# A two-part transformer kernel on one core: gate and modulation work split and counted through, and stages that begin with the high part of h

## The reference

```python
for i in range(DEPTH):                      # first stack, 2 layers
    a = rms_norm(h, attn_norm[i])
    proj = a @ w_in[i]                      # split: attention, state space and gated linear mixers
    h = h + mix @ w_out[i]
    f = rms_norm(h, ffn_norm[i])
    h = h + (silu(f @ w_ffn_gate[i]) * (f @ w_ffn_up[i])) @ w_ffn_down[i]
    h = h + sigmoid(h @ ple_w_gate[i]) * (p[i] @ ple_w_proj[i])
c_act = silu(c)
for i in range(DEPTH_2):                    # second stack, 4 layers
    mod = c_act @ ada_w[i] + ada_b[i]       # 1024 x 6144, a matrix-vector product
    sh1, sc1, g1, sh2, sc2, g2 = split(mod, 6)
    h = rms_norm(x, norm_gain[i, 0]) * (1.0 + sc1) + sh1
    x = x + g1 * attention_i(h)             # stick-breaking, block, sliding window, stick-breaking
    h = rms_norm(x, norm_gain[i, 1]) * (1.0 + sc2) + sh2
    x = x + g2 * swiglu(h, ffn_w_gate[i], ffn_w_up[i], ffn_w_down[i])
```

## Time and profile before

| | |
|---|---|
| runs | 2368.3, 2370.2, 2378.3 us; median 2370.16 us |
| the profiled execution | 2372.31 us, of which the span from first to last instruction is 2370.5 us |
| mean granted clock of TensorE | 0.971 of 2.4 GHz |
| TensorE busy | 2210.4 us (93%), 17460 matmul records |
| DVE, ACT busy | 1573.5 us (66%), 1072.2 us (45%) |
| moved from memory | 433.82 MB, 183 GB/s over the span |

### The profile page before, as it was taken

One profiled execution on the slowest core, in us unless ns is written; L12 is line 12 of the kernel. 1 busy time (PEld: TensorE's weight loads), 2 busy tenths in 40 slices (PEclk: granted clock), 3 DMA queues, 4 the chain that ended last, 5 costly groups with the idle time before them and its releaser, 6 DMA issues.

```text
span 2370.5 us, 44905 instructions
## 1 busy us (share of the span) xinstructions
PE 2210.4 (93%) x17460; PEld 2080.8 (88%) x17460; DVE 1573.5 (66%) x2623; ACT 1072.2 (45%) x1728; POOL 0.2 (0%) x4
## 2 busy tenths in 40 slices
PE   5889999898999999999899999899988999998998
PEld 4778899877888999799899888799877999897998
DVE  4676678726766888366788766778777555676554
ACT  3545444324454443255444445544455444555443
POOL 0000000000000000000000000000000000000000
PEclk7999999999999999899999999999999999999999
DMA  4465399834552998454599753599842565542764
GB/s 119 110 161 159 112 301 292 270 111 122 156 152 88 304 303 281 123 160 132 160 296 305 242 147 113 169 297 301 262 116 90 160 186 168 143 142 76 206 188 142
DMA packets 549150, 436.34 MB, mean 184 GB/s; under 512 B 27664, under 2 KB 475192, under 8 KB 548920
## 3 DMA queue, kind: packets, MB, share of 16 engines
q1 hardware_dynamic: 545680, 431.22, 59.8%
q10 hardware_dynamic: 3368, 3.71, 0.5%
HBM read 433.82 MB, written 1.05 MB: 183 GB/s over the span
## 4 chain that ended last, share of the span: by engine, by line
PE 80%; DVE 9%; ACT 4%; DMA 2%; DVEq 2%; issue 1%; ACTq 1%; SPq 0%
PE bank L633 14%; PE bank L635 13%; PE bank L634 13%; PE acc L633 7%; PE acc L635 6%; PE acc L634 6%; PE bank L1225 3%; PE bank L756 3%; PE bank L1133 2%; PE bank L816 2%; PE bank L643 1%; ACT w_hi L1258 1%; DVE head_work L1666 1%; DVE w_lo L1691 1%; PE bank L826 1%
## 5 line engine op out<-in xcount | busy, mean ns | idle before, releaser
L633 PE MATMUL bank<-h_hi,w_hi 128*128 128x256 f32 x3024 | 862.3, 285 | 26.8 <-DVE w_lo L1685 9.9
L634 PE MATMUL bank<-h_lo,w_hi 128*128 128x256 f32 x3024 | 843.8, 279 | 0.0
L635 PE MATMUL bank<-h_hi,w_lo 128*128 128x256 f32 x3024 | 843.7, 279 | 0.0
L1258 ACT ACTIVATE w_hi<-wslot 128x1024 fp32r<-128x1024 f32 x574 | 594.0, 1055 | 508.4 <-PE acc L635 265.9
L1691 DVE TENSOR_TENSOR w_lo<-wslot,w_hi 128x1024 fp32r<-128x1024 f32 x396 | 475.1, 1221 | 224.5 <-ACT w_hi L1258 223.9
L633 PEld LDWEIGHTS bank<-h_hi,w_hi 128*128 128x128 f32 x3024 | 569.8, 188 | 54.5 <-DVE w_lo L1685 15.9
L634 PEld LDWEIGHTS bank<-h_lo,w_hi 128*128 128x128 f32 x3024 | 573.7, 190 | 2.3 <-issue 1.7
L635 PEld LDWEIGHTS bank<-h_hi,w_lo 128*128 128x128 f32 x3024 | 570.9, 189 | 0.0
L633 PE MATMUL acc<-mid_hi,w_hi 128*128 128x256 f32 x1120 | 316.9, 283 | 4.3 <-DVE mid_lo L2032 3.3
L635 PE MATMUL acc<-mid_hi,w_lo 128*128 128x256 f32 x1120 | 312.3, 279 | 0.0
L634 PE MATMUL acc<-mid_lo,w_hi 128*128 128x256 f32 x1120 | 312.3, 279 | 0.0
(11 more groups left out here) (274 smaller groups left out, 2629.0 us busy)
## 6 DMA issues: line engine op xcount, KB each, us to landing
wslot<-in_ada_w_dram SPq DMA_DIRECT2D x192, 512.0 KB, 5.9
wslot<-in_ffn_w_gate_dram SPq DMA_DIRECT2D x88, 512.0 KB, 4.8
wslot<-in_ffn_w_up_dram SPq DMA_DIRECT2D x88, 512.0 KB, 5.4
wslot<-in_ffn_w_down_dram SPq DMA_DIRECT2D x88, 512.0 KB, 3.7
wslot<-in_w_in_dram SPq DMA_DIRECT2D x72, 512.0 KB, 5.0
wslot<-in_sb_w_in_dram SPq DMA_DIRECT2D x48, 512.0 KB, 4.6
wslot<-in_w_ffn_gate_dram SPq DMA_DIRECT2D x44, 512.0 KB, 4.8
wslot<-in_w_ffn_up_dram SPq DMA_DIRECT2D x44, 512.0 KB, 5.5
```

The lines of the kernel that those rows point to most:

```text
L633: pe.matmul(dst, w_hi[:, w, cols], hi, start=start, stop=False, skip_group_check=True)
L634: pe.matmul(dst, w_hi[:, w, cols], lo, start=False, stop=False, skip_group_check=True)
L635: return pe.matmul(dst, w_lo[:, w, cols], hi, start=False, stop=stop, skip_group_check=True)
L1258: return act.activation(dst, src, ACT.Copy)
```

## The change

- Modulation blocks are numbered through over all four layers, 48 in all. Each `ffn` does 11 (`ADA_STEPS`) until they are used up: 11, 11, 11, 11, 4 and 0. The phases `ada_units` and `ada_end` are gone; a phase `modulation` after each `ffn`'s add stores the last block and makes `mod_gain`.
- The gate products are split like the others. The eight gate units come in slots 0, 1, 8 and 9, the projection weights as two whole units in slots 2 and 3. The first two gate units and both projection units are loaded ahead of the last gate and up unit of `ffn`, p is turned inside `ffn` too, and the first two gate units are split at its end. In the gate stage TensorE does all projections first, into the four banks, then the gate tiles into `acc`; the first two tiles go along together as quarters of h are split. Each tile is added to `xT` as it is ready.
- At the start of every attention and every `ffn` the first tiles go along together, tile of h by tile of h, and for each the products with the high part come first, on `h_high`, and those with the low part after, on `h_parts`.

```diff
+PLE_SLOTS = (0, 1, 8, 9, 0, 1, 8, 9)
+PLE_PARTS = (0, 1, 3, 4, 2, 0, 1, 3)
+def ada_blocks(ada):
+    return max(0, min(ADA_STEPS, DEPTH_2 * ADA_BLOCKS - ADA_STEPS * ada))
...
+            def first_tiles(g, tiles):
+                for k in range(KT):
+                    pe.wait_ge(sem["h_high"], g("h_high") - KT + k + 1)
+                    for dst, part, first in tiles:
+                        pe.matmul(dst, w_hi[:, part, k_cols(k)], h_hi[:, k, :], start=(first and k == 0), stop=False, skip_group_check=True)
+                        pe.matmul(dst, w_lo[:, part, k_cols(k)], h_hi[:, k, :], start=False, stop=False, skip_group_check=True)
+                    pe.wait_ge(sem["h_parts"], g("h_parts") - KT + k + 1)
+                    for n, (dst, part, _) in enumerate(tiles):
+                        mm = pe.matmul(dst, w_hi[:, part, k_cols(k)], h_lo[:, k, :], start=False, stop=(k == KT - 1), skip_group_check=True)
...
-                project(0, 0)
-                project(0, 1)
+                first_query(g)
...
-                elif kind == "ada_end":
-                    ada_sum(ph["start"], ADA_BLOCKS - 1)
...
-                        for k in range(KT):
-                            mm = pe.matmul(B(2 * b, 0, 256), wk(s, k), xT[:, k, :], start=(k == 0),
-                                           stop=(k == KT - 1))
+                    for m in range(KT):
+                        if m == KT - 2:
+                            pe.wait_ge(sem["ada_stored"], g("ada_stored"))
+                        for n in range(2):
+                            mm = pe.matmul(B(m // 2, 256 * (m % 2), 256 * (m % 2) + 256), wk(SLOT_PROJ + n, m),
+                                           qk[:, 256 * n:256 * n + 256], start=(n == 0), stop=(n == 1))
...
+                        mm = three(acc[:, 2 * (m % 4) + m // 4, :], PLE_PARTS[m], k_cols(k), h_hi[:, k, :], h_lo[:, k, :],
+                                   k == 0, k == KT - 1)
...
+                    for k in range(KT):
+                        if k % 2 == 0:
+                            pe.wait_ge(sem["h_parts"], g("h_parts") + k + 2)
+                        gate(0, k)
+                        gate(1, k)
...
-                    with dve.Fori(0, KT // 2) as i:
+                    for m in range(KT):
+                        gated = silu_g[:, m % 2, :]
+                        dve.wait_ge(sem["ple_s"], g("ple_s") + m + 1)
+                        dve.tensor_tensor(gated, gated, B(m // 2, 256 * (m % 2), 256 * (m % 2) + 256), ALU.mult)
+                        dve.drain()
+                        last = dve.tensor_tensor(xT[:, m, :], xT[:, m, :], gated, ALU.add)
```

More of the change, by code:

```diff
@@ L137, in mix_prior, with runs @@
     return max([v for v in range(u) if mix_part(v) == mix_part(u)], default=None)
+def runs(kinds, lo):
+    ends = [i for i in range(lo + 1, len(kinds)) if kinds[i] != kinds[i - 1]]
+    return list(zip([lo] + ends, ends + [len(kinds)]))
 def grouping(att, n):
@@ L2226, in _, with step @@
                     ada = ph["ada"]
-                    def step(f, b, i, more=True, waits=True, first=False):
+                    def step(f, b, i, more=True, waits=True, first=False, block=True):
                         count = g("w_high") - 3
@@ L2237, in step @@
                         dve.tensor_tensor(mid_lo[:, b, :], mid[:, b, :], mid_hi[:, b, :], ALU.subtract).then_inc(sem["mid_ready"], 1)
[L2238 removed]
+                        if block:
                             for n in range(2 * b, 2 * b + 2):
                                 ada_unit(at, ada, i, n, waits)
+                    blocks = ada_blocks(ada)
                     for b in range(2):
[L2243 to L2246 removed]
@@ new lines, in _ @@
+                    for lo, hi in runs([(i < blocks, i == blocks) for i in range(NF // 2 - 1)], 1):
+                        with dve.Fori(lo, hi) as i:
+                            for b in range(2):
+                                step(2 * i + b, b, i, block=lo < blocks)
+                            if lo == blocks:
+                                ada_store(at, ada, blocks - 1)
+                    for b in range(2):
+                        step(NF - 2 + b, b, NF // 2 - 1, more=b == 0, block=blocks == ADA_STEPS)
@@ new lines, in _ @@
+                    for m in range(2 if ph["stack"] == 1 else 0):
+                        low(PLE_SLOTS[m], PLE_PARTS[m], ph["next"]["w_high"] + m + 1)
+                elif kind == "modulation":
+                    n = ph["ada"]
+                    if ada_blocks(n) == ADA_STEPS:
+                        ada_store(ph["start"], n, ADA_STEPS - 1)
+                        dve.drain()
+                    for c in range(2 if n else 0):
+                        w = 32 + 8 * (2 * (n - 1) + c)
+                        stt(mod_gain[:, n - 1, c, :], mod[:, n - 1, 8 + 24 * c:16 + 24 * c], 1.0, pcol[:, 0, w:w + 8], ALU.add, ALU.mult)
```

273 lines of the change are left out of this document (132 added, 141 removed).

## The result

| | us |
|---|---|
| before, runs beside it (4) | 2372.25 median |
| after (4) | 2339.69 median, 2335.83 to 2345.8 |
| ratio | 0.9863, 95% interval 0.9829 to 0.9897 |
| after once more, other chip (e8, 6 runs) | 0.9875, 0.9854 to 0.9896 |
| profiled execution of after | 2342.8, span 2341.0 |

The time lies in the range given, but above the forecast's own. 32.6 us were saved where 45.4 were forecast, and 29.7 us on the other chip (before 2369.6, after 2339.9).

A forecast was written before the change was run, and what follows sets the result against it. TensorE was taken as the bound, 80% of the chain that ends last. Terms 33 - 5 + 10.6 + 3.6 + 7 - 3.8 = 45.4 us, off the 2370.2 us median, gave 2325; own range 2314 to 2336, range given 2309 to 2345.

The forecast's parts named there:

- two gate stages: Stages between first feed-forward block and next layer, both layers: split matmuls replace float32 ones, saving 33 us.
- early loads, transposes: End of the feed-forward block before each gate stage: four loads moved there lose 2.4 us a layer, 5 in all.
- attention starts: Starts of the six attention stages: query and key tiles going along together save 10.6 us.
- blocks out of two starts: Two attention starts: the vector engine leaves out a modulation block, saving 1.8 us each, 3.6 in all.
- blocks out of two ends: Ends of the same two stages: additions no longer follow a block's sum, saving 3.5 us each, 7 in all.
- four blocks in the fifth stage: Fifth feed-forward stage: four modulation blocks it did not have cost 0.95 us each, 3.8 us lost.
- TensorE has the modulation sum and 12 of the 16 projection matmuls to do in that time: Gate stage start: TensorE has this work during the vector engine's chain, so it stands still little over a microsecond at a time.
- they are issued in the pause: Before the last feed-forward gate unit: four loads find slots free and go out in SP's pause; the unit lands 4.8 us late.
- first rival: Early loads lose 4.8 us a layer and bring half clock, 11 us less saved: 2336 us; chance 0.14.
- second rival: Attention starts do not pay because the next wait ends as now, so 10.6 us vanish: 2336 us; chance 0.08.
- The loops' rate changes: Feed-forward loops: all at the slow rate, 2341 us (chance 0.08), or the other way, as far as 2312 (0.05).
- forecast's own signs of being wrong: Gate stage over 36 us, TensorE's stop over 5 us, or a feed-forward stage grown by more than the four blocks.

The follow-up runs named there:

- e8: The kernel after unchanged, run once more on another chip beside e7: 2339.92 us, ratio 0.9875.
- e3: The kernel after with the second half of the projection of p left out (8 of 16 float32 matmuls in each gate stage): 2336.23 us, ratio 0.9864.
- e1: The kernel after with the four early loads spread one at a time before iterations 2, 4, 6 and 8 of the feed-forward loop: 2328.12 us, ratio 0.9849.
- e4: The kernel after with the first query and key tiles of the six attention stages in the old order, queries first: 2343.48 us, ratio 0.9898.
- e9: The kernel before with three 64-column bfloat16 matmuls once in the fifth and once in the sixth feed-forward loop: 2368.49 us, ratio 1.0.
- e10: The kernel after with three 64-column bfloat16 matmuls once in the fifth and once in the sixth feed-forward loop: 2332.25 us, ratio 0.9853.
- e2: The kernel after with the fifth and sixth feed-forward loops cut into two-iteration pieces, one-column matmuls between those of the sixth: 2340.88 us, one run.
- e7: The kernel of e1 with three 64-column bfloat16 matmuls once in the fifth and once in the sixth feed-forward loop: 2328.30 us, ratio 0.9826.
- e11: The kernel of e7 with the scalar engine taking the squares before the two weight copies in the norms behind the gate stages: 2321.45 us, ratio 0.9805.

## Why the forecast was right in direction, and its saving 13 us too large

| term | forecast | measured | by |
|---|---|---|---|
| two gate stages | 33 | 27.6 | traces; e3 for the cause |
| early loads, transposes | -5 | -9.4 | traces, e1 |
| attention starts | 10.6 | 8.7 | traces, e4 |
| blocks out of two starts | 3.6 | 3.7 | traces |
| blocks out of two ends | 7 | 7.0 | traces |
| four blocks in the fifth stage | -3.8 | -5.0 | traces |
| sum | 45.4 | 32.6 | |

That the sum is the 32.6 of the medians is luck to the last us or two: the other chip has 29.7, e9 and e10 have 36, and the profiled executions, from which the terms are read, differ by 29.5. In them is the pace of the loops (some 3 us won in the first block, 1.5 in the fifth, 6.5 lost in the sixth), and half-clock stretches came and went at places that no term names.

- **Gate stage.** Right: no half clock, tiles 2.83 us apart in the first layer and 2.72 in the second (2.77 forecast; the two paces), the end behind the last sigmoid as worked out (3.6 us). Wrong is the step "TensorE has the modulation sum and 12 of the 16 projection matmuls to do in that time, so it stands still for little more than a microsecond". No duration was put beside those matmuls. The projection takes 7.15 us and the sum 0.9: 8.1 us, where the vector engine's chain was given 5.6. e3 shows both: with half of it gone the gate starts 2.3 us earlier and meets the vector engine; the 2.4 and 1.9 us that it wins are 4.3 of the 5.4 missing in this term. Both stages are under the 36 us that would have refuted the forecast. Of the other traces with this gate stage one, the second layer of e2, has a stretch of half clock at its beginning and takes 36.6 us.
- **Early loads.** The step that failed is "they are issued in the pause". The distance in time was put at 4.8 us for the gate unit alone; it landed at 450.30, which is 451.5 on the old scale (the last sum in the loop starts at 438.8 there, at 437.6 here), close to the 451 forecast, and the first stop is 2.9 us (2.4 forecast, 3.6 in the second layer). What was left out is what comes behind it: in the first layer the up unit took 8.8 us to land and a later down unit brought another stop of 1.6; in the second, 1.7 us went to the half clock behind the stop. The upper bound, 4.8 a layer, was the truth. That is the first rival, with its half clock in one layer of after and in eight of twelve over all traces, but 3.4 us long, and so 1.7 us dear where the rival had 3. By the Trainium skill (DMA: Bandwidth & Descriptors, "Queues, rings and completion order") descriptors are taken up in ring order; the trace agrees, since the gate and the up unit behind the 2 MB landed 7.5 and 8.8 us after their issue, and that was the reading to follow.
- **Starts.** Keys within 1.2 us of the last low part (1.4 in the second layer) where a microsecond was forecast, and 2.0 to 2.3 and 1.0 us a stage as worked out. Wrong was to give the first layer what the second showed: there the keys wait for the scalar engine anyway. Of the second rival only that one stage is true.
- **Ends.** In the block stage the vector engine has now, behind its last weight split (timeline; the earlier trace rows before):

```profile
1465.81 1.23 DVE L1734 TENSOR_TENSOR w_lo<-wslot,w_hi 128x1024 fp32r<-128x1024 f32 x1 [0.52 <-ACT w_hi L1284]
1466.95 3.22 DVE L1708 SCALAR_TENSOR_TENSOR xT<-acc,mod,xT 128x256 f32<-128x256 f32 x8
```

  The additions follow right behind, as forecast: 1.14 us from split to additions instead of 4.01. The squares then start 2.7 us earlier in both stages (2.9 was the lower bound). The part for the half clock, 0.6 a stage, came in one of them and larger: behind the block stage's squares before has 3.4 us at half clock, from 1501.1, after has none, and the first gate product follows 6.93 us behind the first square instead of 8.76. A norm without half clock on either side (the two first-stack ones) gains 0.25 of this, 6.92 for 7.17, so 1.6 are the clock's. In the window stage it is 8.67 for 8.93. Of eleven traces with the changed order six have the block stage's norm at 6.9, so this part is not sure in every run. 2 x 2.7 + 1.6 is 7.0: the sum was right, its parts were not.
- **Four blocks.** 0.95 us a block came from two stages whose loops ran at unlike paces (the third at both in turn, the fifth at 117.8), and it spreads over the blocks what a stage with blocks pays once. The four cost 3.7 for their sums and 1.3 for the stop ahead of the first round.
- **Pace.** "The loops' rate changes" was a rival with a chance of 0.13 and neither of its forms came: each loop has its own pace in each run. But one of the forecast's own signs of being wrong did come by it: a feed-forward stage, the sixth, has grown without any block. e8 shows that this is not the change. The scatter is less with the two loops fixed for before (8.6 us against 21 on one chip); for the kernels with the change it is less clear (6.0, 7.4 and 10.0 in e7, e10 and e11; 17.1, 10.0 and 9.5 in e1, after and e8). With both fixed the saving is 34 to 36 us, so at most a few us of the shortfall are the pace's, and some 10 stay, for the most part with the projection and the loads.

## What to carry to other kernels

Before a stall is written off as hidden, put a duration beside everything that the engine does in it: 7.15 us of projection stood in no sum. A load moved ahead of another one delays those behind it, the second as well as the first, and the stop that it makes can bring a stretch of half clock with it; give it a place where the queue is not about to be waited for, one at a time. And where single runs of one kernel lie 10 us apart, compare stages of traces before totals.

## What had not been expected of the hardware

- Equal 256-column matmuls run at 113.3 or 117.8 ns with the clock granted in full. Inside a loop the pace was seen to hold until something else came: a shorter matmul, a stop, once one more 256-column matmul at a cut. Three 64-column bfloat16 matmuls led to the fast one in all twelve cases seen. Which pace a loop begins with differs between executions of one kernel (the sixth loop: 117.8 in after, 113.3 in e8). Why there are two stays open.
- Of twelve stops of TensorE in which it was idle for 1.8 to 3.6 us, behind the early loads, eight were followed by 3.4 us at a granted clock of 0.5 and four by full clock; the idle times of the two kinds overlap (1.8 to 2.6 us without, 2.2 to 3.6 with it).
- Issuing a load of 512 KB took SP itself 0.4 us, but 1.2 and 1.9 us each for the gate and projection units above, which came in a row with the DMA engines busy.
- The half-clock stretches moved with the change: the mean granted clock rose from 0.971 to 0.979, and the second stick-breaking stage, which had gained 1.0 us at its start, lost it again when a stretch of half clock fell into its next projection (147.2 us, 146.9 before). By stretch, after:

```profile
2008.00:2011.40 3.40, 3.40 (x17) 3.40 (x18) 2.72 (x6) 1.86 (x4) 0.00 (x0) 0.52 1.11 348
```
